# Loading the expert weights of a mixture-of-experts layer by pairs of experts instead of one expert at a time

## What is computed

```python
def routed_experts(h, idx, wts, w1, w3, w2):
    ...
    def expert_group(args):
        tok, wt, e = args
        xb = h_pad[tok]
        hid = jax.nn.silu(xb @ w1[e]) * (xb @ w3[e])
        return (hid @ w2[e]) * wt[:, None]
    ...
y = (jax.nn.silu(h @ ws1) * (h @ ws3)) @ ws2 + routed_experts(h, idx, wts, w1, w3, w2)
```

## Time and profile before

| What | us |
|---|---|
| median of 3 runs (1316.28 to 1318.08) | 1316.66 |
| the profiled execution, its own time | 1306.64 |
| its span in the trace | 1304.9 |
| first `up` of pair 0, start | 618.0 |
| `up` of pair 31, the last, start | 1235.8 |
| busy time of PE, DVE, ACT, POOL over the span | 1023.1, 428.7, 239.5, 217.9 |

### The profile page before, as it was taken

One profiled execution on the slowest core, in us unless ns is written; L12 is line 12 of the kernel. 1 busy time (PEld: TensorE's weight loads), 2 busy tenths in 40 slices (PEclk: granted clock), 3 DMA queues, 4 the chain that ended last, 5 costly groups with the idle time before them and its releaser, 6 DMA issues.

```text
span 1304.9 us, 23540 instructions
## 1 busy us (share of the span) xinstructions
PE 1023.1 (78%) x8385; PEld 652.9 (50%) x8386; DVE 428.7 (33%) x815; ACT 239.5 (18%) x478; POOL 217.9 (17%) x361
## 2 busy tenths in 40 slices
PE   4899999966785799983787778787877887756865
PEld 3898878855664344532344444344433444433432
DVE  4533343448643113783411111111121112101118
ACT  3322223325454000120011111110100111100110
POOL 0011000002200000101222222222232232212211
PEclk9899999979898899996789899989898999988988
DMA  9575545456272991185679699987999988899955
GB/s 349 171 255 184 186 131 183 169 187 221 75 268 68 327 277 65 45 362 155 234 269 385 251 398 394 364 293 300 406 374 388 335 305 303 327 397 402 404 211 233
DMA packets 97815, 347.50 MB, mean 266 GB/s; under 512 B 14961, under 2 KB 20129, under 8 KB 73050
## 3 DMA queue, kind: packets, MB, share of 16 engines
q1 hardware_dynamic: 81162, 311.56, 64.4%
q0 software_dynamic: 13856, 30.13, 6.9%
q10 hardware_dynamic: 2736, 4.98, 1.1%
HBM read 329.15 MB, written 29.52 MB: 275 GB/s over the span
## 4 chain that ended last, share of the span: by engine, by line
PE 27%; DMA 16%; issue 6%; DVE 2%; SPq 1%; ACT 0%; POOL 0%; POOLq 0%; DVEq 0%; ACTq 0%
PE PS L1826 8%; DMA hT<-h_rows,ixo 7%; DMA W<-w 7%; PE PS L1841 6%; PE PS L1857 4%; PE PS L1882 4%; PE PS L1896 2%; PE PS L1832 1%; DMA vec<-ln_b 1%; PE PS L1814 1%; PE PS L1872 1%; DVE hido L1948 0%; PE PS L1849 0%; DVE hid L1943 0%; DMA W<-expert_rows 0%
## 5 line engine op out<-in xcount | busy, mean ns | idle before, releaser
L1826 PE MATMUL PS<-W,XT 128*32 128x256 f32 x2048 | 128.4, 406 | 51.0 <-DMA W<-w 27.9
L1841 PE MATMUL PS<-W,XTo 128*64 128x256 f32 x1216 | 140.7, 384 | 0.0
L1826 PEld LDWEIGHTS PS<-W,XT 128*32 128x32 f32 x2048 | 79.5, 117 | 115.1 <-issue 90.2
L1841 PEld LDWEIGHTS PS<-W,XTo 128*64 128x64 f32 x1216 | 94.0, 138 | 44.9 <-issue 11.7
L1857 PE MATMUL PS<-W,hidTo 128*64 128x512 f32 x304 | 88.5, 707 | 16.3 <-DVE hidTo L1951 10.7
L306 PE MATMUL PS<-w_hi,u_hi 128*128 128x512 f32 x240 | 94.1, 392 | 1.2 <-DVE w_lo L432 0.7
L306 PE MATMUL PS<-w_hi,u_lo 128*128 128x512 f32 x240 | 93.5, 389 | 0.0
L306 PE MATMUL PS<-w_lo,u_hi 128*128 128x512 f32 x240 | 93.4, 389 | 0.0
L1882 PE MATMUL PS<-W,hidT 128*32 128x512 f32 x512 | 69.3, 654 | 26.8 <-issue 24.9
L432 DVE TENSOR_TENSOR w_lo<-raw,w_hi 128x2048 fp32r<-128x2048 f32 x26 | 59.5, 2289 | 91.9 <-ACT w_hi L372 91.9
L1911 ACT ACTIVATE sg<-PS 64x256 f32<-64x256 f32 x32 | 12.1, 378 | 343.4 <-PE PS L1826 343.4
(11 more groups left out here) (342 smaller groups left out, 1488.6 us busy)
## 6 DMA issues: line engine op xcount, KB each, us to landing
W<-w SPq DMA_DIRECT2D x192, 1024.0 KB, 13.1
raw<-w_in SPq DMA_DIRECT2D x26, 1024.0 KB, 5.3
wada<-w_ada SPq DMA_DIRECT2D x6, 2048.0 KB, 7.6
W<-expert_rows SPq DMA_DIRECT2D x24, 512.0 KB, 12.6
kc<-cache_k_diff SPq DMA_DIRECT2D x8, 512.0 KB, 5.1
vc<-cache_v_diff SPq DMA_DIRECT2D x8, 512.0 KB, 3.6
Wa<-p_a SPq DMA_DIRECT2D x4, 1024.0 KB, 7.4
Wa<-w_out SPq DMA_DIRECT2D x4, 1024.0 KB, 10.0
```

Source lines behind the costliest of these rows:

```text
L1826: mm = pe.matmul(PS[64 * h + 32 * c:64 * h + 32 * c + 32, UP_B + i, 0:F], XT[:, i, k, 32 * c:32 * c + 32], t.W13[:, 2 * i + c, h, k], star ...
L1841: mm = pe.matmul(PS[64 * h:64 * h + 64, XH_B, 0:F], XTo[:, k], t.W13[:, slot, h, k], start=k == 0, stop=k == KD - 1)
```

## The change

The three loads of an expert become three loads of a pair: w1 of both experts in one transfer of 2 MB, w3 of both, w2 of both. The semaphores `wup_in` and `wdown_in` are now two each instead of four, one for a pair. SP waits once in a pair, for the last extra block of c1, before it issues w1 and w3.

```diff
+def of_pair(w, turn, i):
+
+    by_turn = w.rearrange("(s u) p k n -> u s p k n", s=WB)
+    pair = by_turn[turn, 2 * i:2 * i + 2] if isinstance(turn, int) else by_turn[bass.ds(turn, 1), 2 * i:2 * i + 2].rearrange("u s p k n -> (u s) p k n")
+    return pair.rearrange("s p k n -> p s k n")
+
+
+def load_up(sp, t, turn, i):
+
+    for h, w in enumerate((t.w1v, t.w3v)):
+        sp.dma_start(t.W13[:, 2 * i:2 * i + 2, h], of_pair(w, turn, i)).then_inc(t.wup_in[i], 16)
...
                     sp.wait_ge(h_mm, n + 1)
-                    for c in range(2):
-                        used = sp.value_load(t.ov[0:1, bass.ds(n * 2 + (c + 1), 1)], min_val=0, max_val=XB)
-                        sp.wait_ge(o_h, used + 1)
-                        stand_alone(sp)
-                        load_up(sp, t, expert_at(it + 1, 2 * i + c), 2 * i + c)
+                    used = sp.value_load(t.ov[0:1, bass.ds(n * 2 + 2, 1)], min_val=0, max_val=XB)
+                    sp.wait_ge(o_h, used + 1)
+                    stand_alone(sp)
+                    load_up(sp, t, it + 1, i)
                     sp.wait_ge(yy_mm, n + 1)
                     stand_alone(sp)
-                    for c in range(2):
-                        load_down(sp, t, expert_at(it + 1, 2 * i + c), 2 * i + c)
+                    load_down(sp, t, it + 1, i)
...
-                for c in range(2):
-                    pe.wait_ge(t.wup_in[2 * i + c], (it + 1) * 32)
+                pe.wait_ge(t.wup_in[i], (it + 1) * 32)
...
-                    pe.wait_ge(t.wdown_in[slot], (it + 1) * 16)
+                    pe.wait_ge(t.wdown_in[slot // 2], (it + 1) * 16)
...
-                for c in range(2):
-                    pe.wait_ge(t.wdown_in[2 * i + c], (it + 1) * 16)
+                pe.wait_ge(t.wdown_in[i], (it + 1) * 16)
```

More of the change, by code:

```diff
@@ L1397, in router_signals, with load_down @@
         ("ws_in", "eb_in", "r_mm", "sig_done", "placed_done", "s_mm"))
[L1400 to L1417, removed]
+def of_pair(w, turn, i):
[5 more added lines that the diff above has]
+        sp.dma_start(t.W13[:, 2 * i:2 * i + 2, h], of_pair(w, turn, i)).then_inc(t.wup_in[i], 16)
+def load_down(sp, t, turn, i):
+    sp.dma_start(t.W2[:, 2 * i:2 * i + 2], of_pair(t.w2v, turn, i)).then_inc(t.wdown_in[i], 16)
 def routing(nc, t):
@@ L1456, in _ @@
             sp.dma_start(ws2[:, :, :], t.ws2[0].rearrange("(p k) n -> p k n", k=2)).then_inc(ws2_in, 16)
-            for i in range(WB):
-                load_up(sp, t, expert_at(0, i), i)
-                load_down(sp, t, expert_at(0, i), i)
+            for i in range(PW):
+                load_up(sp, t, 0, i)
+                load_down(sp, t, 0, i)
         @block.tensor
@@ L2076, in streaming_layer @@
         t.ident_done = ctx.enter_context(nc.semaphore("ident_done"))
-        t.wup_in = [ctx.enter_context(nc.semaphore(f"wup_in{i}")) for i in range(WB)]
-        t.wdown_in = [ctx.enter_context(nc.semaphore(f"wdown_in{i}")) for i in range(WB)]
+        t.wup_in = [ctx.enter_context(nc.semaphore(f"wup_in{i}")) for i in range(PW)]
+        t.wdown_in = [ctx.enter_context(nc.semaphore(f"wdown_in{i}")) for i in range(PW)]
         t.phase_sems = []
```

## The result

The changed kernel takes **1297.31 us** (median of 4 runs, 1295.78 to 1303.24), beside 1316.47 us for the kernel before (4 runs, 1309.90 to 1318.08): a ratio of 0.9886, 95% interval 0.985 to 0.9921. Measured twice more, each time beside the kernel before on one chip, it gave 0.9906 (0.9872 to 0.9939) and 0.9901 (0.9867 to 0.9935). Some 3 us of the distance to the forecast time may lie in the base: the 1316.66 us came from three runs, and the later medians of the kernel before are 1312.11 to 1314.07. One run of the kernel before was slow (2578.06 us) and is left out of all medians here.

A forecast was written before the change was run, and what follows sets the result against it. The prediction took TensorE's waits for weight loads (27.9 us) and for extra blocks' gathers (25.0 us) to bound the kernel. Its terms, +2 - 5.8 - 5 + 6 - 0.7 = -3.5 us, gave 1313.2 us from 1316.66, range 1306 to 1323.

The forecast's parts named there:

- The moved loads, pairs 4 to 9, +2: Pairs 4 to 9: the burst makes weights late, pair 9 starts 1 to 3 us later, pair 4's 3.15 gain gone: +2 us.
- Pair 10, -5.8: Pair 10: the gather wait of 4.05 us goes and half of 3.4 us of clock loss returns: -5.8 us.
- The forecast's half: Pair 10: only half of the 3.4 us of clock loss counted as won, since the clock also fell elsewhere.
- Pairs 19 to 21, -5: Pairs 19 to 21: gathers meet an emptier queue, and of 5.5 us of waits 5 go: -5 us.
- The end, +6: Last pairs, bound by loads: pair 23's w2 lands later, paid in full at the last pairs: +6 us.
- Smaller ones, -0.7: Ahead of each up: TensorE has one wait less, 51 ns, at most 1.3 us, partly covered: -0.7 us.
- A sign that failed: Expert stage: TensorE's waits for weights rise from 27.9 to about 34 us, all of it in the last pairs.
- The size, 0: Weight loads: a 2 MB transfer takes as long as the second of two 1 MB loads, so 0 us.
- faster transfers: Rival, weight loads: larger transfers move faster, 14 us gained besides the 3.5, about 1299 us; chance 0.06.
- a gather that must let a whole transfer pass: Rival, gathers under load: each waits one MB longer, 2.7 us, waits grow up to 32 us, 1338 us; chance 0.05.
- the band of 390 to 400: Saturated stretches of the DMA engines: rate stays at 390 to 400 GB/s; leaving that band makes the prediction wrong.
- The burst costs more than the gathers give: Rival, pairs 10 and 19 to 23: w2 lands after 22.6 us, gather waits stay, about +7 us, 1323 to 1324; chance 0.20.

The follow-up runs named there:

- e1_move: Kernel before with only c0's w1 and w3 loads moved behind c1's last extra block, 1 MB transfers, separate semaphores: 1305.90 us, 0.9969 of before.
- e3: Kernel before with moved loads and joint semaphores, still 1 MB transfers: 1298.94 us, 0.9907 of before.
- e6_tail: e3, but from pair 23 on c0's w1 and w3 leave ahead of c1's extra blocks again: 1296.79 us, 0.9893 of before.
- e5: Changed kernel with TensorE's waits for weights written twice at each up and each pair's down: 1305.74 us, 0.9932 of before.
- e2: Kernel before with only the semaphores joined, one for a pair; loads in the old order and size: 1307.02 us, 0.9962 of before.
- e10: Joint semaphores alone on the kernel before, as e2, run once for a second profile: 1310.03 us.
- e12_after: The changed kernel again, unaltered, beside e11_unrolled on the same chip: 1299.59 us, 0.9901 of before.
- e4: The changed kernel again, unaltered, for a second profile: 1298.53 us, 0.9906 of before.
- e7_two_loads: Changed kernel with TensorE's queue reading two instead of three extra-block bounds in every second pair: 1296.83 us, 0.9867 of before.
- e11_unrolled: e7_two_loads with TensorE's loop over the pairs written out: 1297.80 us, 0.9904 of before.

## Why the prediction was right or wrong

**The direction and the moved loads came out about as forecast (-2.8 us in the sum, -4 with e1_move, 0.3 to 8); the step that failed is the term of the waits on TensorE, put at -0.7 us, which gave about 5 by itself and 7 on top of the move.** 0.2% was forecast, 1% measured. By its own steps:

*The moved loads, pairs 4 to 9, +2*: +2.5 in the table, an agreement that is worth little, as the two profiles of before are 3.2 us apart there. The late weights are there, but a pair earlier: all four profiles with both edits wait for weights ahead of pair 8's up (1.5 to 3.8 us), and three of them also ahead of pair 9's (0.7 to 4.0 us). In after:

```profile
782.00 5.00 PE L1821 MATMUL PS<-W,XT 128*32 128x256 f32 x64 [3.00 <-DMA W<-w]
...
800.43 3.66 PE L1821 MATMUL PS<-W,XT 128*32 128x256 f32 x64 [2.28 <-DMA W<-w]
```

Neither profile of before waits for weights there. Pair 4 won 1.5 us in the table's means and not 3.15; pair 9's loss of clock is in the row too.

*Pair 10, -5.8*: -5.8, the mechanism right and the last digit luck. The wait is gone (0.9 us is left in e3), and of the clock not half but all came back: the two downs took 3.68 and 3.57 us before and take 1.94 and 1.92 in after. But the slow downs had covered other things. The forecast's half stood for "the clock also fell elsewhere"; what took the other half is a wait for DVE and TensorE's own queue ahead of the next up, which starts 2.56 us after the down in after and started 3.39 us after it before. The pair's down of before, and the transposes of the block's hidden rows in after:

```profile
855.43 3.57 PE L1882 MATMUL PS<-W,hidT 128*32 128x512 f32 x16 [0.80 <-issue]
```

```profile
845.07 0.31 PE L1844 MATMUL PS<-ident,hido 64*128 64x64 f32 x2 [0.55 <-DVE hido L1942]
```

*Pairs 19 to 21, -5*: -5.2, of which some 0.8 belong to the semaphores (the move alone: -4.4).

*The end, +6*: **half wrong**. The mechanism is there. Issues of pair 23 in the timeline of SP of after:

```profile
1110.53 0.89 SPq L1410 DMA_DIRECT2D W<-w  x2
1117.35 0.37 SPq L1415 DMA_DIRECT2D W<-w  x1
```

and the landing of the second:

```profile
W<-w SPq DMA_DIRECT2D x1, 2048.0 KB, 13.6
```

1117.35 + 13.6 - 1110.53 = 20.4 us from the burst's first issue, 0.2 below the 20.6 to 22.6 foreseen. The wait that it causes, ahead of pairs 26 and 27, before and after:

```profile
1152.30 5.35 PE L1826 MATMUL PS<-W,XT 128*32 128x256 f32 x64 [3.43 <-DMA W<-w]
...
1170.12 4.97 PE L1826 MATMUL PS<-W,XT 128*32 128x256 f32 x64 [8.32 <-DMA W<-w]
```

```profile
1143.46 5.18 PE L1821 MATMUL PS<-W,XT 128*32 128x256 f32 x64 [9.21 <-DMA W<-w]
...
1159.32 5.78 PE L1821 MATMUL PS<-W,XT 128*32 128x256 f32 x64 [6.62 <-DMA W<-w]
```

Ahead of pair 26 it is +5.8, the forecast's own figure; ahead of pair 27 it is -1.7 again. What failed here is "paid in full at the last pairs, since nothing has slack behind it". Counted from the up of pair 23, and in the means of the two profiles of before and the four with both edits, the up of pair 26 comes 4.5 us later, that of pair 27 only 2.2, and that of pair 31 still 2.8. So half of the lateness fades between the ups of pairs 26 and 27, and the rest stays to the end. The DMA engines are busy all the time between these two ups in either kernel (share 1.0), so no gap in the queue explains it; why the weights of pair 27 catch up isn't shown. All in all the end costs 2.8 us. e6_tail says the same from the other side.

*Smaller ones, -0.7*: **wrong, and the largest miss.** "TensorE has one wait less ahead of each up: 51 ns" has two errors. The change takes a wait away ahead of each pair's down as well; the diff shows it, though the listing ahead of the prediction shows the up alone. And a wait costs not the length of its row but the distance to the next instruction of the queue, 0.11 to 0.12 us, which e5 shows by adding it back. In the trace of before, ahead of pair 23's up, the row of L1820 starts at 1108.41 us and the next of that queue at 1108.53. That is 0.23 us a pair, 7 us for 32 pairs; where weights are late it turns into a longer wait for them. Measured were 3 to 7 us by e5 against the changed kernel, about 5 (2 to 8) by e2 against the kernel before, and 7 by e3 against e1. The Trainium skill, Perfetto Trace Analysis, Sequencer-only Instruction, says that the profile reports only the execution of such an instruction, and neither its wait for a semaphore nor the time in which its own update spreads; e5 agrees in that a row of 51 ns takes 0.11 us of the queue. Whoever had read the row L1882 <- issue: 23.4 in 28 beside the earlier trace rows would have asked what TensorE's queue does there.

*A sign that failed*: the waits for weights were to rise to about 34 us, all of it in the last pairs. They rose to 40.1 in after, and only 2.5 of these 12.2 us lie ahead of the ups of pairs 26 to 31; the others lie ahead of those of pairs 6, 8, 9 and 18. So TensorE spends part of what it saves elsewhere on waiting for weights.

*Pair 2, not in the sum*: -2.2, by the semaphores alone (33.5 with e2 and e10, 35.7 with e1 and e5). Behind the gather's wait in this pair the granted clock falls to 0.50, which is 1.2 GHz. Windows of that stretch before, and in e12_after:

```profile
671.10:677.90 6.80, 6.37 (x27) 3.04 (x27) 0.98 (x2) 0.59 (x1) 1.34 (x3) 0.50 0.29 99
```

```profile
671.70:675.10 3.40, 3.40 (x14) 1.47 (x12) 0.55 (x1) 0.00 (x0) 0.98 (x1) 0.50 0.32 101
```

It stays down for 6.8 us in all four profiles with two waits and for 3.4 in nine of the ten with one (in the profile of after it doesn't fall there). The wait ahead of it is hardly shorter, 2.6 to 3.0 us with one wait against 2.7 to 3.1 with two. Why the clock comes back earlier was not tried. The same is seen in pair 10 without the move: 10.2 us in both profiles of before, 3.4 in both of the semaphores alone. But over the stage there is no such order: from 650 to 1250 us the mean granted clock is 0.94 in both profiles of before, and 0.92 and 0.95 with the semaphores alone.

*The size, 0, and the rivals*: e3 and e4 agree to 0.4 us, each known to some 4, so neither the 14 us of faster transfers nor the 21 us of a gather that must let a whole transfer pass is there: with 2 MB transfers the gathers wait 14.5 us in 8 (e4), with 1 MB 15.1 in 8 (e3). Where the DMA engines are busy all the time the rate is 397 GB/s from 785 to 829 us in after, beside the 394 of the earlier trace rows; in the last pairs it reaches 425 to 432 in stretches of 4 us in both kernels, so the band of 390 to 400 was no sign of anything. "The burst costs more than the gathers give" fell with the 20.4 us.

What stays open: the single edits add up to 9 us and the two together gave 12, within the intervals. Summed over all pairs, the four profiles with both edits are 3 us shorter than the two with the move alone (from the first up on), and 2.1 of that lie in pair 2, while the times of e1 and e3 are 7 us apart; so the price of a wait is shown, and what the semaphores give the whole kernel is not split up. The profiles of the semaphores alone show that waits for weights take back most of what the queue gives up (34.0 and 34.4 us in place of 27.9 and 28.2), so their 5 us rest on the times and on pair 2, not on a full account. And no version was shown to be faster than the changed kernel: e7_two_loads has the best ratio, 0.9867, but its interval overlaps the others.

## What to carry to other kernels

Read the idle time of the bound engine that no other engine explains, and what its own queue does there, before pricing an instruction off the path: a wait that has long been met costs the distance to the next instruction and not its own row, and a merged transfer can pay through the semaphore it saves rather than through its bytes. Loads that are not urgent can be issued behind a small transfer that the engine waits for: here that halved the waits for gathers (25.0 to 13.0 us), raised those for weights by 11 and won about 4. A loss in a stretch bound by loads is to be followed to the end of the stage: of 4.5 us of lateness ahead of pair 26, 2.2 were left a pair later.

## What the runs showed of the hardware

- A semaphore wait on TensorE's queue that is already met: a row of 51 ns, 0.11 to 0.12 us of TensorE's idle time where its queue ends last (e5_double).
- Loads of 1 MB or of 2 MB: no difference in time that could be told, 1298.94 against 1298.53 us, each known to some 4 us (e3_move_sem, e4_after; the queue holds several loads there).
- The granted clock stayed at 0.50 for 6.8 or for 3.4 us behind nearly the same gather wait in pair 2, 6.8 in all four profiles with two waits for weights ahead of ups and downs and 3.4 in nine of ten with one.
- A written-out loop of 32 pairs on TensorE fetched twice the packets of instructions (80 against 41) and had 7 new stalls, 15.7 us in all, up to 3.4 us each; the kernel was no faster (e11_unrolled 1297.80 us, e12_after 1299.59).
